# Block products of a per-head projection: rounded activations and their low part as one 512-wide moving operand, the two halves of each accumulator added on VectorE

## What is computed

```python
def odd_layer(x, norm_g, w_in, b_forget, w_out):
    h = rmsnorm(x, norm_g)
    q, k, v, gate, f = split(h @ w_in)            # 16 heads x 128 each, f: 16
    cum = cumsum(log_sigmoid(f + b_forget))
    s = q @ k.T / sqrt(128) + cum_q - cum_k       # causal, per head
    o = softmax(s) @ v
    return x + (o * silu(gate)) @ w_out
```

## Time and profile before

| | |
|---|---|
| runs of the kernel | 2948.32, 2948.53, 2949.63 us; median 2948.53 |
| the profiled execution | 2949.23 us, of which the span is 2947.4 us and 1.8 us lie around it |
| PE busy | 2888.1 us (98%), PEld 2430.1 (82%) |
| DVE / ACT / POOL busy | 1539.2 (52%) / 1333.6 (45%) / 1410.3 (48%) |
| mean granted TensorE clock | 0.995 of full speed |
| stretch of the block products | about 2052 to 2745 us of the span, 15 units |
| L2187 (w_lo on POOL) | 298 instructions, 435.0 us, mean 1537 ns on arena and 1422 ns on raw |

### The profile page before, as it was taken

One profiled execution on the slowest core, in us unless ns is written; L12 is line 12 of the kernel. 1 busy time (PEld: TensorE's weight loads), 2 busy tenths in 40 slices (PEclk: granted clock), 3 DMA queues, 4 the chain that ended last, 5 costly groups with the idle time before them and its releaser, 6 DMA issues. The chain is left out here.

```text
span 2947.4 us, 52822 instructions
## 1 busy us (share of the span) xinstructions
PE 2888.1 (98%) x20478; PEld 2430.1 (82%) x20478; DVE 1539.2 (52%) x2031; ACT 1333.6 (45%) x1858; POOL 1410.3 (48%) x1031
## 2 busy tenths in 40 slices
PE   8999999999999999999999999999999999999998
PEld 6777777777787887778787777887999999999886
DVE  7556655434444117778733335118666666666412
ACT  5434434245565323333434554325555555556422
POOL 1223322433324544667743334544566666666643
PEclk9999999999999999999999999999999999999999
DMA  5111111222212443222242223442232323332433
GB/s 219 60 60 59 52 56 55 90 82 80 78 57 85 165 139 100 97 90 96 86 147 93 91 88 111 162 138 80 97 107 104 110 96 106 104 108 98 161 125 114
DMA packets 98561, 298.17 MB, mean 101 GB/s; under 512 B 10608, under 2 KB 16880, under 8 KB 97408
## 3 DMA queue, kind: packets, MB, share of 16 engines
q1 hardware_dynamic: 71440, 246.12, 24.5%
q10 hardware_dynamic: 26992, 50.22, 5.2%
HBM read 273.45 MB, written 22.84 MB: 101 GB/s over the span
## 5 line engine op out<-in xcount | busy, mean ns | idle before, releaser
L3416 POOL TENSOR_TENSOR w_lo<-raw,w_hi 128x512 fp32r<-128x512 f32 x624 | 844.6, 1376 | 1217.2 <-ACT w_hi L768 1216.1
L338 PE MATMUL ps<-act_hi,w_hi 128*128 128x512 f32 x1232 | 486.4, 395 | 10.8 <-POOL w_lo L3416 5.0
L768 ACT ACTIVATE w_hi<-raw 128x1024 fp32r<-128x1024 f32 x316 | 333.6, 1056 | 357.3 <-PE ps L340 135.3
L339 PE MATMUL ps<-act_hi,w_lo 128*128 128x512 f32 x1232 | 481.0, 390 | 0.0
L340 PE MATMUL ps<-act_lo,w_hi 128*128 128x512 f32 x1232 | 480.9, 390 | 0.0
L2187 POOL TENSOR_TENSOR w_lo<-arena,w_hi 128x512 fp32r<-128x512 f32 x150 | 227.5, 1537 | 183.0 <-ACT w_hi L2110 183.0
L1035 PE MATMUL ps<-act_hi,w_hi 128*128 128x512 f32 x736 | 294.2, 400 | 0.0
L338 PEld LDWEIGHTS ps<-act_hi,w_hi 128*128 128x128 f32 x1232 | 231.9, 188 | 72.7 <-issue 16.1
L1036 PE MATMUL ps<-act_hi,w_lo 128*128 128x512 f32 x736 | 286.9, 390 | 0.0
L1037 PE MATMUL ps<-act_lo,w_hi 128*128 128x512 f32 x736 | 286.7, 390 | 0.0
L2093 PE MATMUL ps<-act_hi,w_hi 128*128 128x256 f32 x960 | 274.2, 286 | 2.1 <-POOL w_lo L2187 2.1
(11 more groups left out here) (501 smaller groups left out, 5895.8 us busy)
## 6 DMA issues: line engine op xcount, KB each, us to landing
raw<-stream SPq DMA_DIRECT2D x378, 512.0 KB, 3.3
arena<-stream SPq DMA_DIRECT2D x64, 512.0 KB, 3.3
residual<-mix ACTq DMA_DIRECT2D x32, 256.0 KB, 2.0
arena<-residual ACTq DMA_DIRECT2D x32, 256.0 KB, 2.7
arena<-x_rows SPq DMA_DIRECT2D x4, 1024.0 KB, 18.3
arena<-x ACTq DMA_DIRECT2D x16, 256.0 KB, 2.7
kept_qk<-mix ACTq DMA_DIRECT2D x16, 256.0 KB, 2.0
arena<-kept_qk ACTq DMA_DIRECT2D x16, 256.0 KB, 3.8
```

The lines of the kernel that those rows point to most:

```text
L338: pe.matmul(dst, w_hi[:, slot, j, :], act_hi[:, a, :], start=first, stop=False)
L339: pe.matmul(dst, w_lo[:, slot, j, :], act_hi[:, a, :], start=False, stop=False)
L768: nc.scalar.activation(w_hi[:, s, :, :], src[:, s % 2, :, :], ACT.Copy).then_inc(cast_done, 1)
L3416: last = nc.gpsimd.tensor_tensor(w_lo[:, s, part, :], raw[:, s % 2, part, :], w_hi[:, s, part, :].bitcast(F32), ALU.subtract)
```

## The change

Four things are edited.

1. **Products.** The rounded block and its low part become one moving operand of 2 x 256 columns. For each of the 8 steps there is one matmul of w_hi on both (512 columns, into both halves of the bank) and one of w_lo on the rounded part (256 columns, into the first half). 24 matmuls a product become 16, and 3 weight loads a step become 2.
2. **Sums.** Each accumulator is then 128x512, and the result is the sum of its halves. The copies x1, x5, x2, c21 and the sums c12, c22, c11 become 512 wide, and DVE gets four new additions a pair, f12, f22, f11, f21: each 128x256, both inputs in SBUF (f11, f12 and f22 behind the sum of the same name; f21 behind ACT's c21). f21 of pair 0 stands after T2 of pair 1; f21 of pair 1 stands in the next unit after T2 and ahead of decayed. The transpose vt waits for f21 (before: c11 and c21), and ACT's x2 waits for f21 of the pair before.
3. **Places.** So that one access pattern reaches both parts, act_hi and act_lo are one tensor, mix and arena are one, and the rounded s3 and s4 move; h3 now waits for l4, and the loads of the mixed tiles 8 to 14 at the end wait for product 4 of the last pair instead of 3.
4. **After the loop,** DVE does f21 of the last pair ahead of out3_rest and out3_vector.

```diff
-        act_hi = sb("act_hi", [P, KT, T], F32R)
-        act_lo = sb("act_lo", [P, KT, T], F32R)
-        with nc.sbuf_tensor("mix_r", [P, KT * T], F32R) as rounded:
-            mix_r = rounded
-        mix = sb("mix", [P, KT * T])
+        acts = sb("acts", [P, 2 * KT * T], F32R)
+        act_hi, act_lo = (slots(acts, KT * j, KT).rearrange("p (k t) -> p k t", k=KT) for j in range(2))
+        with nc.sbuf_tensor("cells_r", [P, (KT + 30) * T], F32R) as rounded:
+            cells_r = rounded
+        cells = sb("cells", [P, (KT + 30) * T])
+        mix, mix_r = (slots(view, 0, KT) for view in (cells, cells_r))
+        arena, arena_r = (slots(view, KT, 30) for view in (cells, cells_r))
...
-        s_hi = {"1": eight(arena_r, 26), "2": eight(arena_r, 18), "3": half_k(act_hi[:, low_k, :], 1),
-                "4": half_k(act_lo[:, low_k, :], 1)}
+        s_hi = {"1": eight(arena_r, 26), "2": eight(arena_r, 18), "3": half_k(mix_k_r[:, high_k, :], 0),
+                "4": half_k(act_hi[:, low_k, :], 1)}
         s_lo = {"1": half_k(mix_k_r[:, high_k, :], 1), "2": half_k(mix_k_r[:, low_k, :], 0),
-                "3": half_k(mix_k_r[:, low_k, :], 1), "4": half_k(mix_k_r[:, high_k, :], 0)}
-        w7_acts = ((half_k(act_hi[:, low_k, :], 0), half_k(act_lo[:, low_k, :], 0)),
-                   (s_hi["1"], s_lo["1"]),
-                   (s_hi["2"], s_lo["2"]),
-                   (s_hi["4"], s_lo["4"]),
-                   (s_hi["3"], s_lo["3"]),
-                   (half_k(act_hi[:, high_k, :], 0), half_k(act_lo[:, high_k, :], 0)),
-                   (half_k(act_hi[:, high_k, :], 1), half_k(act_lo[:, high_k, :], 1)))
+                "3": half_k(mix_k_r[:, low_k, :], 1), "4": half_k(act_lo[:, low_k, :], 1)}
+        def every_half(first, half):
+
+            return [2 * first + 2 * j + half for j in range(HK)]
+
+        def every(first):
+
+            return [2 * first + j for j in range(HK)]
+
+        act_halves, cell_halves = (view[:, :].rearrange("p (s t) -> p s t", t=HT) for view in (acts, cells_r))
+        w7_places = ((act_halves, every_half(0, 0), every_half(KT, 0)),
+                     (cell_halves, every(KT + 26), every_half(HK, 1)),
+                     (cell_halves, every(KT + 18), every_half(0, 0)),
+                     (act_halves, every_half(0, 1), every_half(KT, 1)),
+                     (cell_halves, every_half(HK, 0), every_half(0, 1)),
+                     (act_halves, every_half(HK, 0), every_half(KT + HK, 0)),
+                     (act_halves, every_half(HK, 1), every_half(KT + HK, 1)))
+
+        def w7_hi_of(i, j):
+
+            view, hi, _ = w7_places[i]
+            return view[:, hi[j], :]
+
+        def w7_both(i, j):
+
+            view, hi, lo = w7_places[i]
+            first, second = sorted((hi[j], lo[j]))
+            return view[:, first:second + 1:second - first, :]
...
-            if name in "34":
+            if name == "4":
                 act.wait_ge(pe_half, 2 * (N_ODD + 3) + 1)
+            elif name == "3":
+                fold_dve.wait(act, f"l4{q}", 0)
...
-        w7_out = Steps(sem("w7_out"), "c12 c22 c11")
+        w7_out = Steps(sem("w7_out"), "c12 f12 c22 f22 c11 f11 f21")
...
-            return ps[:, pp, 0:HT], ps[:, 1 - pp, 0:HT]
+            return ps[:, pp, :], ps[:, 1 - pp, :]
...
-                sp.wait_ge(w7_pe, 7 * last + 4)
+                sp.wait_ge(w7_pe, 7 * last + 5)
...
-            hi, lo = w7_acts[i]
+            halves = dst.rearrange("p (a t) -> p a t", a=2)
             first = i in (0, 1, 5)
             for j in range(HK):
-                pe.matmul(dst, w_hi[:, slot, j, :], hi[:, j, :], start=first and j == 0, stop=False,
+                pe.matmul(halves, w_hi[:, slot, j, :], w7_both(i, j), start=first and j == 0, stop=False,
                           skip_group_check=True)
-                pe.matmul(dst, w_lo[:, slot, j, :], hi[:, j, :], start=False, stop=False, skip_group_check=True)
-                mm = pe.matmul(dst, w_hi[:, slot, j, :], lo[:, j, :], start=False, stop=j == HK - 1,
+                mm = pe.matmul(dst[:, 0:HT], w_lo[:, slot, j, :], w7_hi_of(i, j), start=False, stop=j == HK - 1,
                                skip_group_check=True)
...
+                if not first_pair(u, pp):
+                    w7_out.wait(act, "f21", p - 1)
                 w7_part.mark(nc.scalar.activation(x2, b, ACT.Copy), name)
             else:
                 act.wait_ge(w7_pe, p * 7 + 7)
-                w7_part.mark(nc.scalar.activation((at_q_in, at_v_in)[pp][:, HT:T], b, ACT.Copy, scale=scale), name)
+                w7_part.mark(nc.scalar.activation(x2, b, ACT.Copy, scale=scale), name)
...
-            second = (at_k_in, at_gate)[pp]
+            first, second = ((at_q_in, at_k_in), (at_v_in, at_gate))[pp]
+            add = nc.vector.tensor_tensor
             if name == "c12":
                 w7_out.start(p)
                 if pp:
                     dve.wait_ge(mixed_stored, u * 16 + 16)
                 w7_part.wait(dve, "x2", p)
                 dve.wait_ge(w7_pe, p * 7 + 4)
-                w7_out.mark(nc.vector.tensor_tensor(second[:, 0:HT], d, x2, ALU.add), name)
+                w7_out.mark(add(second, d, x2, ALU.add), name)
+            elif name == "f12":
+                w7_out.wait(dve, "c12", p)
+                w7_out.mark(add(second[:, 0:HT], second[:, 0:HT], second[:, HT:T], ALU.add), name)
             elif name == "c22":
                 dve.wait_ge(w7_pe, p * 7 + 5)
-                w7_out.mark(nc.vector.tensor_tensor(second[:, HT:T], b, x5, ALU.add), name)
-            else:
+                w7_out.mark(add(x5, b, x5, ALU.add), name)
+            elif name == "f22":
+                w7_out.wait(dve, "c22", p)
+                w7_out.mark(add(second[:, HT:T], x5[:, 0:HT], x5[:, HT:T], ALU.add), name)
+            elif name == "c11":
                 dve.wait_ge(w7_pe, p * 7 + 6)
                 w7_out.mark(nc.vector.scalar_tensor_tensor(
-                    out=(at_q_in, at_v_in)[pp][:, 0:HT], in0=d, scalar=1.0 if pp else ODD_SCALE, in1=x1,
-                    op0=ALU.mult, op1=ALU.add), name)
+                    out=first, in0=d, scalar=1.0 if pp else ODD_SCALE, in1=x1, op0=ALU.mult, op1=ALU.add), name)
+            elif name == "f11":
+                w7_out.wait(dve, "c11", p)
+                w7_out.mark(add(first[:, 0:HT], first[:, 0:HT], first[:, HT:T], ALU.add), name)
+            else:
+                w7_out.wait(dve, "f11", p)
+                w7_part.wait(dve, "c21", p)
+                w7_out.mark(add(first[:, HT:T], x2[:, 0:HT], x2[:, HT:T], ALU.add), name)
                 w7_out.finish()
...
-                    w7_out.wait(pe, "c11", at_pair(u, -1))
-                    w7_part.wait(pe, "c21", at_pair(u, -1))
+                    w7_out.wait(pe, "f21", at_pair(u, -1))
...
-                w7_out.wait(act, "c22", at_pair(u, 1))
+                w7_out.wait(act, "f22", at_pair(u, 1))
...
                 prepare(u, par, 0, "T2")
                 if not (isinstance(u, int) and u == 0):
+                    w7_sum_out(dve, u - 1, 1, "f21")
                     decayed(u)
                 prepare(u, par, 0, "l2")
                 if isinstance(u, int) and u == 0:
@@ -2449,13 +2485,15 @@
                 largest(u)
                 prepare(u, par, 0, "T4")
                 scaled(u)
-                w7_sum_out(dve, u, 0, "c12")
-                w7_sum_out(dve, u, 0, "c22")
+                for name in ("c12", "f12", "c22", "f22"):
+                    w7_sum_out(dve, u, 0, name)
                 turned(u)
                 prepare(u, par, 1, "T1")
                 w7_sum_out(dve, u, 0, "c11")
+                w7_sum_out(dve, u, 0, "f11")
                 prepare(u, par, 1, "l1")
                 prepare(u, par, 1, "T2")
+                w7_sum_out(dve, u, 0, "f21")
                 prepare(u, par, 1, "l2")
                 gated(u, at_gate)
                 prepare(u, par, 1, "T3")
@@ -2467,14 +2505,15 @@
                         V.wait(dve, names[j], u)
                     return mark
 
-                w7_part.wait(dve, "c21", at_pair(u, 0))
+                w7_out.wait(dve, "f21", at_pair(u, 0))
                 split(at_q_in, at_q, at_q_lo, done(("qh", "qc")))
                 split(at_k_in, at_k, at_k_lo, done(("kh", "kc")))
-                w7_sum_out(dve, u, 1, "c12")
-                w7_sum_out(dve, u, 1, "c22")
+                for name in ("c12", "f12", "c22", "f22"):
+                    w7_sum_out(dve, u, 1, name)
                 if not last:
                     prepare(u + 1, 1 - par, 0, "T1")
                 w7_sum_out(dve, u, 1, "c11")
+                w7_sum_out(dve, u, 1, "f11")
                 if not last:
                     prepare(u + 1, 1 - par, 0, "l1")
...
             V.start(u)
+            w7_sum_out(dve, u - 1, 1, "f21")
             out3_rest(dve, range(2))
```

(7 more changed lines are left out.)

## The result

The changed kernel takes 2970.86 us (median of 4 runs, 2969.22 to 2971.63) against 2948.43 for the kernel before (4 runs, 2947.97 to 2949.63). The ratio is 1.0074, 95% interval 1.0062 to 1.0087: 22.4 us slower, where 25 was forecast.

A forecast was written before the change was run, and what follows sets the result against it. A DVE, ACT and POOL loop was taken to set the pace after the change: units +25.9, start -1.4, slack -2.0, end +2.8, sum +25.3 on 2949.2; less 0.7 for the median, 2974 us, range 2950 to 2990.

The forecast's parts named there:

- A loop through DVE, ACT and POOL just behind PE: Block products: closed loop T1, l1, T2, l2, T3, ACT, POOL, T1 without a product; own pace 45.0 to 45.3 a unit.
- The lock inside the loop: A DVE operation with two SBUF inputs and a POOL piece exclude each other for their whole length and take turns.
- PE's saving: Matmul steps: 0.360 falls to 0.347, 13 ns saved, 1.5 us a unit, 22 us over 15 units.
- rival A: PE keeps the pace and the additions are hidden: 2928, or 2944 at the loop's own pace; chance together 0.15.
- f12 and f22: Additions where POOL works towards T1's piece: each holds POOL 0.25 (0 to 0.43), 1.0 a unit.
- f21 behind T2: In pair 0, f21 waits 1.25 for POOL's piece and works 0.33; decayed starts 6.3 after T1.
- Start: Start of the block products: l40 and l41 run alone, POOL's l3 moves behind them: -1.4 (-3 to +3).
- Slack used up: Last unit: PE has 1.8 in hand between POOL's last piece and product 6; loss starts only after that: -2.0.
- End: After the last pair, f21 waits for c21 and holds up low parts, w_lo, vt and output projection: +2.8 (0 to +4.5).
- B: Rival: f21 slips in behind T2 before POOL's turn; unit 46.3, about 2957; chance 0.15.
- C: Rival: PE's clock falls in the new wait ahead of vt, product 1 1.5 longer: 2989; chance 0.08.
- D: Rival: the two effects cancel, f12 and f22 nearly free and the lock wait half: 2945 to 2953; chance 0.06.

The follow-up runs named there:

- e2: The kernel before plus four additions a pair of the same size at the places of f12, f22, f11, f21, into an unread scratch tile: 2976.21 us, ratio 1.0095.
- e1: The changed kernel without the four additions f12, f22, f11, f21; wide products, copies and sums stay: 2937.48 us, ratio 0.9961 against the kernel before.
- e8: The changed kernel with f12, f22, f11 as reduces, f21 partly from PSUM and moved, last f21 later, POOL's product 3 waiting for T2: 2937.01 us.
- e3: The changed kernel with all four additions as a tensor_reduce with one SBUF input instead of two: 2950.29 us, ratio 1.0006 against the kernel before.
- e5: The changed kernel with only f12 and f22 as a tensor_reduce; f11 and f21 stay two-input additions: 2961.78 us, ratio 1.0045 against the kernel before.
- e7: e2 plus one wait: POOL does not begin product 3's low part before T2 is done: 2946.32 us, ratio 0.9994 against the kernel before.
- e9: The changed kernel plus one wait: POOL begins product 3's low part only after T2: 2945.68 us, ratio 0.9992 against the kernel before.
- e4: The changed kernel with only f21 as a tensor_reduce; f12, f22 and f11 stay two-input additions: 2956.11 us, ratio 1.0024 against the kernel before.
- e6: The changed kernel with the last f21 moved behind the output projection's first low parts and w_lo: 2968.98 us, ratio 1.0071 against the kernel before.

## Why the prediction was right

2974.0 was forecast and 2970.9 measured, inside the range and on the side that had 0.75. By its steps:

- **A loop through DVE, ACT and POOL just behind PE.** Right in what decides: e2 lengthens that loop with PE's work unchanged, and the unit goes from 45.60 to 47.47. Its own pace, put at 45.0 to 45.3, was too long: e1 and e8 run at 44.86 and 44.83 with PE almost without a gap, so the loop needs no more than that there. The profile also shows PE idle for 1.3 a unit, 1.1 of it ahead of vt, where 3.3 and 1.7 were forecast, and none of the short waits for POOL's w_lo.
- **The lock inside the loop.** Right, and shown by e3 to e5 and by e7 and e9.
- **PE's saving.** Too high: 13 ns a step were forecast. The timeline shows 0.351 for a step in mid-product (9 ns). Where one product follows another there is next to no saving (the last step of one and the first of the next take 0.359 and 0.366 in e1, 0.361 and 0.360 before), and the mean of all steps from 2150 to 2650 is 0.3549 in e1 against 0.3614 before, 6.5 ns, times 112 steps 0.73 a unit. e1's 0.74 is the same by T1. The forecast's sum did not use it, rival A's 2928 did: with all additions hidden, e8 gives 2937. The gap figure of the Trainium skill (TensorE: Matmul & The Clock Gate, Back-to-back issue gap), columns/2.4 + 2.5 ns, is 0.109 and 0.216; that section gives it for an isolated matmul. The trace shows 0.118 and 0.233 for this alternation, so it doesn't hold here.
- **Wider copies.** Right: c12, c22, c11 0.69 (0.68 forecast), ACT's c21 0.58, T2 ahead of POOL in all pairs after the first (1.22 to 1.23).
- **f12 and f22.** This is the term that was mis-sized: I took 0.25 of POOL's time for each; 1.0 a unit. By e5 they cost 0.54 a unit (e3 against e4: 0.46, f11 included). Pair 0 was 23.71 instead of 23.95, pair 1 23.29 instead of 23.5. A unit came out at 47.00 instead of 47.45, 6 us over 14 units.
- **f21 behind T2.** Right in detail: forecast 1.25 + 0.33 and decayed 6.3 after T1; measured 1.50 and 6.35. The sum had it at 0.90 in pair 0 (23.45 against 22.55) and 0.25 in pair 1; by e4 it costs 0.80 and 0.18, 0.98 a unit.
- **Start.** -1.4 forecast, -0.8 in the first unit. The +2.8 ahead of it was not forecast; it lies within what this start varies by from one profiled execution to another.
- **Slack used up.** Right as far as it can be seen: from the last T1 to the last s the last unit's +1.85 and the slack's -2.0 make -0.15; measured -0.6, which is what the unit's true +1.40 gives with the same -2.0; no run tests the slack by itself.
- **End.** +2.8 forecast, +3.3 measured; e6 shows the mechanism and its price, 3.1.
- **The sum.** Forecast and measured, in the order of the stretches: ahead of the first T1 0 and +2.8, first unit -1.4 and -0.8, units 1 to 13 +24.1 (13 of 1.85) and +17.7, last T1 to last s -0.15 and -0.6, end +2.8 and +3.3: 25.3 and 22.4. The unit term was 6.4 too high, and the variable start hides 2.8 of that: so much of the closeness, 3 us, is luck.

The rivals. A (PE keeps the pace, additions hidden) did not come, but it is possible, in e8, at PE's true price. B (f21 slips in behind T2) did not come in the changed kernel and is what e7 and e9 do, where POOL is held by a wait of its own: 2945.7, and I had priced it at 2957. C (the clock): it stays at 1.00 in the loop from the second unit on, although PE waits for f21 in every unit (1.2 at most in one piece), and falls to half only in the output projection's first microseconds, behind waits of 2.79 and 1.89 (window with 0.63 above; half until 2777). No cost of that was separated out. D did not come.

## What to carry to other kernels

Where an engine is busy without a gap, look for the chain through the others that has just as little slack, before you price what a cheaper instruction there brings; here the saving could be at most 11 us and the other chain took back three times that. A small DVE operation with two SBUF inputs is not priced by its own length when GpSimd works on SBUF: it is priced by whether a GpSimd piece is already waiting when it comes, so give it one input, put it where GpSimd stands still, or hold GpSimd back by a wait on the DVE operation ahead of it. And an addition queued behind a step that others wait for delays all of them: the last f21 cost 3 us, moved down by two calls.

## What the hardware showed that I had not expected

- **A wait that makes a kernel faster by 25 to 30 us.** A semaphore wait added to POOL, on an operation that the lock made it wait for anyway (after 2970.86, e9 2945.68; e2 2976.21, e7 2946.32). A GpSimd piece that already stands at the lock gets in between two DVE operations issued back to back (f21 1.50); one that has to wait for a semaphore of the first starts 0.16 after the second of them (e7, e9: f21 0.42).
- **The lock's price for the loop is smaller than the DVE operation.** A 256-wide addition of 0.42 us alone puts off POOL's pieces towards T1 by about 0.14 (an estimate: e5's 0.54 a unit, for four).
- **The PE step in a mix.** 256-wide matmuls alone follow at 0.120, 512-wide alone at 0.227; alternating, the 512-wide one takes 0.233 and the 256-wide one 0.118.
